# A two-layer hybrid trunk on one core: another opening and order of the recurrent stage, and attention by query blocks with its steps spread over two heads

## What is computed

```
x = x + recurrent_block(rmsnorm(x), ...)          # layer 0
x = x + sq_relu_mlp(rmsnorm(x), w1, w2)           # d_ff = 4096
kv = rmsnorm(x) @ w_kv                            # shared K and V
x = x + diff_attention(rmsnorm(x), w_q, ..., k, v)   # layer 1
x = x + sq_relu_mlp(rmsnorm(x), w1, w2)
return rmsnorm(x)
```

```
# recurrent_block: xy = h @ w_in + b_in, split in xb and yb
xc = conv4(xb) + conv_b;  r, i = sigmoid(block-diagonal matmuls of xc)
a = exp(-8 r softplus(-lam));  bx = sqrt(1 - a*a) * (i * xc)
hs = scan(a, bx);  return (hs * gelu(yb)) @ w_out
# diff_attention: 8 heads, q and k have two halves of 64 rows, v has 128
s = q k^T / 8 + ALiBi bias, causal;  p = softmax(s)
w = p[half 0] - lam * p[half 1];  o = w @ v
o = rmsnorm(o, subln_g, eps) * (1 - lam_init);  return o @ w_o
```

## Time and profile before

| | us |
|---|---|
| median of 3 runs | 1158.46 (1155.45 to 1159.59) |
| the profiled execution | 1158.65 |
| its span, first to last instruction | 1156.8 |
| PE busy | 1109.6 |
| DVE busy | 613.1 |
| ACT busy | 472.9 |
| POOL busy | 108.4 |

### The profile page before, as it was taken

How to read it: one execution, slowest core, us unless ns; L and a number is a source line. 1 busy time by engine, 2 the same in 40 slices (tenths; PEclk the granted TensorE clock), 3 DMA queues, 4 the chain that set the end, 5 groups by cost and what they waited for, 6 DMA issues and landing times.

```text
span 1156.8 us, 13824 instructions
## 1 busy us (share of the span) xinstructions
PE 1109.6 (96%) x4854; PEld 883.9 (76%) x4854; DVE 613.1 (53%) x940; ACT 472.9 (41%) x731; POOL 108.4 (9%) x95
## 2 busy tenths in 40 slices
PE   8999999999999999999999899889999999999995
PEld 4676788888888888888866566668888888888884
DVE  4676965434434434446477877866433433433434
ACT  5475754313313313434246456654422322322342
POOL 0000021000000000021013322322000000000023
PEclk8999999999999999999999999999999999999998
DMA  5222232332322232233221111123223223223322
GB/s 206 73 73 73 73 110 92 99 102 91 97 103 91 92 107 91 92 108 107 76 74 37 54 37 54 37 73 100 101 92 109 92 91 106 94 91 101 98 73 73
DMA packets 30293, 102.42 MB, mean 89 GB/s; under 512 B 3248, under 2 KB 5552, under 8 KB 30128
## 3 DMA queue, kind: packets, MB, share of 16 engines
q1 hardware_dynamic: 29968, 100.74, 26.1%
q10 hardware_dynamic: 288, 1.18, 0.3%
HBM read 99.81 MB, written 2.10 MB: 88 GB/s over the span
## 4 chain that ended last, share of the span: by engine, by line
PE 83%; DVE 10%; ACT 4%; issue 2%; DMA 1%; SPq 0%; DVEq 0%; ACTq 0%
PE ps L1249 73%; PE ps L1380 4%; ACT prob L663 2%; PE ps L1443 1%; DVE prob L1140 1%; DVE w_lo L780 1%; DVE prob L1137 1%; PE ps L1417 1%; PE ps L1308 1%; DVE lru_v L874 1%; DVE inv_lam L1135 1%; ACT w_hi L430 1%; PE ps L1313 1%; DVE lru_v L907 1%; DMA w_raw<-weights 1%
## 5 line engine op out<-in xcount | busy, mean ns | idle before, releaser
L430 ACT ACTIVATE w_hi<-w_raw 128x1024 fp32r<-128x1024 f32 x184 | 193.6, 1052 | 240.9 <-PE ps L1249 205.3
L1249 PE MATMUL ps<-h_hi,w_hi 128*128 128x512 f32 x704 | 287.9, 409 | 2.9 <-DVE w_lo L780 2.9
L1249 PE MATMUL ps<-u_hi,w_hi 128*128 128x512 f32 x696 | 279.9, 402 | 4.2 <-DVE u_lo L918 1.9
L1249 PE MATMUL ps<-h_hi,w_lo 128*128 128x512 f32 x704 | 278.0, 395 | 0.0
L1249 PE MATMUL ps<-h_lo,w_hi 128*128 128x512 f32 x704 | 277.6, 394 | 0.0
L1249 PE MATMUL ps<-u_hi,w_lo 128*128 128x512 f32 x696 | 271.1, 390 | 0.0
L1249 PE MATMUL ps<-u_lo,w_hi 128*128 128x512 f32 x696 | 271.0, 389 | 0.0
L780 DVE TENSOR_TENSOR w_lo<-w_raw,w_hi 128x1024 fp32r<-128x1024 f32 x176 | 216.7, 1231 | 29.6 <-ACT w_hi L430 29.5
L1249 PEld LDWEIGHTS ps<-h_hi,w_hi 128*128 128x128 f32 x704 | 134.4, 191 | 36.8 <-DVE w_lo L780 4.6
L1249 PEld LDWEIGHTS ps<-u_hi,w_hi 128*128 128x128 f32 x696 | 130.7, 188 | 37.8 <-issue 5.9
L1249 PEld LDWEIGHTS ps<-h_lo,w_hi 128*128 128x128 f32 x704 | 134.5, 191 | 31.8 <-issue 4.7
(11 more groups left out here) (163 smaller groups left out, 885.1 us busy)
## 6 DMA issues: line engine op xcount, KB each, us to landing
w_raw<-weights SPq DMA_DIRECT2D x184, 512.0 KB, 3.3
x<-x_t SPq DMA_DIRECT2D x8, 256.0 KB, 7.3
y_t<-att SPq DMA_DIRECT2D x8, 256.0 KB, 2.3
gw<-gate_weights ACTq DMA_DIRECT2D x1, 1024.0 KB, 5.4
lam_in<-lam_vecs ACTq DMA_DIRECT2D x1, 128.0 KB, 2.4
vec<-vectors SPq DMA_DIRECT2D x1, 64.5 KB, 4.1
```

The costliest lines, as they stand in the source:

```text
L430: nc.scalar.activation(w_hi[:, t % RING, :], w_raw[:, t % RAWS, :], ACT.Copy).then_inc(whi_done, 1)
L1249: ins = nc.tensor.matmul(ps[:, bank, :], w[:, slot, ws], o[:, k, :], start=(k == 0 and n == 0), stop=(k == NCH - 1 and n == 2))
```

## The change

Opening: `vec` is loaded from ACT's queue, and `gw` only after all chunks of `h_hi`. Tiles 0 and 1 are loaded and split in halves, interleaved with `x` chunks 0 and 1. Two of the four unused matmuls remain. The squares are added on DVE (`first_sum`), and one matmul in the middle of tile 2 adds over partitions.

Recurrent stage: the same work per chunk, in another order on ACT and DVE; gates come later among the tiles; nine more table loads on ACT. Tiles 16 to 23 split their weights before the residual add (`early=True`).

Attention: scores are one float32 product for all widths, `kq` isn't split. `combined` makes P0 + ratio P1 (ratio = -lam total0/total1) in three instructions, without the division of P0, since the norm behind it takes out a row's scale; the epsilon is scaled to match (`variance`). `attend` runs per query block with the probabilities as weights and V's 128 columns as moving data, reads V in place, and gives rows of queries; the squares are summed by ACT (`squares`), Newton runs on 128x4 on DVE, ACT scales the rows and PE turns them back with four transposes (`back`). POOL has no work here. The steps are spread: `transposes` 2 and 3, `attend` and the norm of head h-1 run during head h. All heads are written out, without loops. SBUF names: `att_hi`, `att_lo` hold the attended heads.

```
-WARM_UP = 4
+WARM_UP = 2
...
+            load_x(0)
+            load_half(0, 0)
+            load_half(1, 0)
+            load_x(1)
+            load_half(0, 1)
+            load_half(1, 1)
+            for m in range(2, NCH):
+                load_x(m)
             with sp.Fori(1, TILES // RAWS) as i:
                 for slot in range(RAWS):
...
+            nc.scalar.dma_start(gw[:, :], gate_weights).then_inc(gw_in, 16)
+            split_hi(2)
+            for m in range(4):
+                first_square(m)
+            split_hi(3)
             act.wait_ge(decay_done, 1)
             nc.scalar.activation(small[:, 1, :], small[:, 0, :], ACT.Exp, scale=-1.0).then_inc(decay_done, 1)
-            split_hi(3)
-            act.wait_ge(consts_done, 1)
-            norm_guess(N_A)
-            nc.scalar.preload_act_table_set("sigmoid_and_others")
+            for m in range(4, NCH):
+                first_square(m)
+            nc.scalar.dma_start(lam_in[:, :], lam_vecs).then_inc(lam_loaded, 16)
...
+            def scaled(h):
+                act.wait_ge(sub_rstd, h + 1)
+                if h:
+                    act.wait_ge(back_mm, h)
+                for j in range(QB):
+                    ins = nc.scalar.activation(o_rows[:, rows(j)], ps[:, BANK_O, rows(j)], ACT.Copy,
+                                               scale=o_stats[:, h % 2, 4, j:j + 1])
+                ins.then_inc(o_scaled, 1)
+            def attended_hi(h):
+                act.wait_ge(back_mm, h + 1)
+                nc.scalar.activation(att_hi[:, h, :], ps[:, BANK_T, :], ACT.Copy,
+                                     scale=lam_s[:, 6:7]).then_inc(ohi_done, 1)
...
+            def first_sum(m):
+                dve.wait_ge(sq_done, m + 1)
+                if m > 1:
+                    dve.wait_ge(sum_done, m - 1)
+                nc.vector.tensor_tensor(acc[:, :], work[:, 0, :] if m == 1 else acc[:, :],
+                                        work[:, m % 4, :], ALU.add).then_inc(sum_done, 1)
...
+            split_lo(4)
             decay()
             norm_newton(N_A)
             dve.wait_ge(conv_consts, 1)
+            split_lo(5)
             branch(0)
+            split_lo(6)
             branch(1)
+            branch(2)
             conv(0)
-            split_lo(4)
-            branch(2)
+            branch(3)
             conv(1)
+            split_lo(7)
+            branch(4)
...
+                dve.wait_ge(exp_done, QB * h + j + 1)
+                own.step(nc.vector.reciprocal(inv[:, s:s + 1], total[:, h % 2, j, 1:2]))
+                own.wait()
+                own.step(nc.vector.scalar_tensor_tensor(
+                    out=ratio[:, s:s + 1], in0=inv[:, s:s + 1], scalar=neg_lam,
+                    in1=total[:, h % 2, j, 0:1], op0=ALU.mult, op1=ALU.mult))
+                own.wait()
+                nc.vector.scalar_tensor_tensor(out=prob[:, s, 0, 0:n], in0=prob[:, s, 1, 0:n],
+                                               scalar=ratio[:, s:s + 1], in1=prob[:, s, 0, 0:n],
                                                op0=ALU.mult, op1=ALU.add).then_inc(prob_done, 1)
...
+                nc.vector.scalar_tensor_tensor(
+                    out=o_stats[:, h % 2, 1, :], in0=o_stats[:, h % 2, 0, :], scalar=1.0 / V_DIM,
+                    in1=o_stats[:, h % 2, 3, :], op0=ALU.mult, op1=ALU.add).then_inc(var_done, 1)
...
             for _ in range(WARM_UP):
@@ -1322,18 +1326,24 @@
             for k in range(NCH):
                 for t in range(2):
                     if k == 0:
-                        tile_starts(t, 0)
+                        pe.wait_ge(first_lo, t + 1)
+                    elif k == NCH // 2:
...
-            gates_after = {2: (0,), 3: (1,), 4: (2,), 5: (3,), 7: (4,), 8: (5,), 10: (6,), 11: (7,)}
+            gates_after = {4: (0,), 5: (1, 2), 6: (3,), 7: (4,), 9: (5,), 10: (6,), 12: (7,)}
...
+                    if t == 2 and k == NCH // 2:
+                        pe.wait_ge(sum_done, NCH - 1)
+                        nc.tensor.matmul(ps[:, BANK_STATS, :], ones[:, :], acc[:, :], start=True,
+                                         stop=True).then_inc(stats_done, 1)
...
-                if n == P:
-                    products = ((kq, kq),)
-                for m, (q, k) in enumerate(products):
-                    for c in range(2):
-                        rows = slice(c * HEAD_DIM, (c + 1) * HEAD_DIM)
-                        ins = nc.tensor.matmul(ps[:, BANK_SCORES + 2 * (j % 2) + c, 0:n],
-                                               q[rows, 1, qb * P:(qb + 1) * P], k[rows, 0, 0:n],
-                                               start=(m == 0), stop=(m == len(products) - 1))
+                    pe.wait_ge(bank_read, T_QK + 2 * h + 2)
+                if a >= 2:
+                    pe.wait_ge(scores_read, 2 * (a - 1))
+                for c in range(2):
+                    rows = slice(c * HEAD_DIM, (c + 1) * HEAD_DIM)
+                    ins = nc.tensor.matmul(ps[:, BANK_SCORES + 2 * (j % 2) + c, 0:n],
+                                           kq[rows, h % 2, 1, qb * P:(qb + 1) * P],
+                                           kq[rows, h % 2, 0, 0:n], start=True, stop=True)
...
+                pe.wait_ge(prob_done, a + 1)
+                if a >= 1:
+                    pe.wait_ge(trans_read, a)
+                if h and j == 2:
+                    pe.wait_ge(olo_done, O_ATT + h)
...
+            def attend(h, j):
+                a = QB * h + j
+                qb = QB - 1 - j
+                pe.wait_ge(trans_read, a + 1)
+                if h and j == 0:
+                    pe.wait_ge(o_scaled, h)
+                for kb in range(qb + 1):
+                    ins = nc.tensor.matmul(ps[:, BANK_O, qb * P:(qb + 1) * P],
+                                           prob_t[:, j % 2, kb * P:(kb + 1) * P],
+                                           value[:, kb, h * P:(h + 1) * P], start=(kb == 0),
+                                           stop=(kb == qb))
                 ins.then_inc(att_mm, 1)
-            def sub_sum(h, i):
-                pe.wait_ge(att_read, at(h + 1, i, 2))
-                bank = BANK_T if h == HEADS - 1 else BANK_O
...
+            def back(h):
+                pe.wait_ge(o_scaled, h + 1)
+                pe.wait_ge(trans_read, min(QB * (h + 1) + 2, QB * HEADS))
+                for qb in range(QB):
+                    qs = slice(qb * P, (qb + 1) * P)
+                    ins = nc.tensor.transpose(ps[:, BANK_T, qs], o_rows[:, qs], ident[:, :])
+                ins.then_inc(back_mm, 1)
...
+            for h in range(HEADS - 1):
+                kq_part(h + 1, 0)
+                scores(h, 0)
+                if h:
+                    transposes(h - 1, 2)
+                    attend(h - 1, 0)
+                scores(h, 1)
+                if h:
+                    attend(h - 1, 1)
+                kq_part(h + 1, 1)
+                scores(h, 2)
+                if h:
+                    transposes(h - 1, 3)
+                kq_part(h + 1, 2)
+                if h:
+                    attend(h - 1, 2)
+                    attend(h - 1, 3)
+                kq_part(h + 1, 3)
+                transposes(h, 0)
+                kq_part(h + 1, 4)
+                transposes(h, 1)
+                kq_part(h + 1, 5)
+                scores(h, 3)
+                kq_part(h + 1, 6)
+                if h:
+                    back(h - 1)
+                kq_part(h + 1, 7)
+            h = HEADS - 1
```

More of the change, by code:

```diff
@@ L707, in attended_hi @@
[L707 to L717 removed]
+                n = (QB - j) * P
+                act.wait_ge(trans_mm, a + 1)
@@ new lines, in _ @@
+            h = HEADS - 2
+            biased(h, 3)
+            halved(h)
+            query(h + 1)
+            combined(h, 2)
+            key(h + 1)
+            attended_lo(h - 1)
+            combined(h, 3)
+            split_lo(T_QK + 2 * h + 1 + RING)
+            h = HEADS - 1
+            biased(h, 0)
+            biased(h, 1)
+            combined(h, 0)
+            split_lo(T_QK + 2 * h + RING)
+            variance(h - 1)
+            biased(h, 2)
+            combined(h, 1)
+            sub_newton(h - 1)
```

762 lines of the change are left out of this document (343 added, 419 removed).

## The result

| | before, us | after, us |
|---|---|---|
| median of 4 runs each | 1156.95 | 1108.82 (1108.08 to 1109.4) |
| span of the profiled execution | 1156.8 | 1107.1 |
| opening, up to tile 2 | 31.9 | 19.2 |
| tiles 2 to 23 | 145.2 | 135.7 (with one statistics matmul, 0.87) |
| attention, the stretch of the earlier trace rows | 187.0 | 159.7 |

The ratio is 0.958 (95% interval 0.956 to 0.961). Against the profiled execution of before, 1158.65 us, the median is 49.8 us shorter. The forecast was 44.5 shorter, 1114 us. The traces place all of it: 22.5 us are gone at the start of the first MLP (177.32 us before, 154.84 after) and 27.3 in attention; everything between and behind has its old length within 0.1 us. The second stretch of the earlier trace rows ends at 177.10, with the last pass ahead of the MLP; to the MLP's start it is 145.4 us, so tiles 2 to 23 are 9.7 us shorter in the table's terms and not 9.5.

A forecast was written before the change was run, and what follows sets the result against it. PE, busy nearly all of the span, was taken to set the time, with gains in its waits and needless work: 1158.65 - 10.5 (opening) - 9.5 (tiles 2 to 23) - 24.5 (attention) = 1114 us, range 1107 to 1131.

The forecast's parts named there:

- likeliest case: Whole kernel: all gains come with small failures on both sides, 1108 to 1120 us, chance 0.56.
- Opening: Start up to tile 2: first pass at about 6.9 us, 31.9 us becomes 20.5 + 0.9, gain 10.5 us.
- cold start: Tiles 0 and 1: PE's first passes run at a lowered clock after idling, costing 2 to 3.4 us.
- so it isn't the bound: Opening: DVE delivers h_lo of chunk 7 by about 14 us, so PE isn't held by it.
- hidden behind tile 1 and the start of tile 2: Opening: DVE's seven sums, 0.69 us each, finish before the one statistics matmul left in tile 2.
- Tiles 2 to 23: Recurrent stage: later gates and the new order leave 2 us of waits, 145.2 becomes 135.7 us, gain 9.5.
- Attention: Attention stretch: 187.0 us becomes 154.4 + 4.6 + 3.5 = 162.5, gain 24.5 us.
- 1: Attention scores: the float32 halves run one behind the other, 17 us more, 1131 us; chance 0.11.
- 2: Recurrent stage: bound by ACT and DVE in turn, half to all of 9.5 us lost, 1119 to 1124; chance 0.14.
- 3: Attention: the norm's chain binds each head, 1 to 2 us late, giving 1121 to 1128 us; chance 0.12.
- 4: Attention: slower than before, as transposes and `back` share one bank; PE's period above 25 us; chance 0.02.
- 5: Opening: vec's small rows still land near 7 us, 3.5 us come back, 1118 us; chance 0.03.

The follow-up runs named there:

- `same_rows`: The kernel after with both halves of the attention scores computed from the same 64 rows of query and key; 1126.2 us, in a single execution.
- `more_loads`: The kernel after with eleven more loads of ACT's function table in the recurrent stage, ahead of the sigmoids; 1112.94 us, in a single execution.
- `warm_0`: The kernel after without the two unused matmuls at the start; 1108.85 us (1108.28 to 1109.2).

## Why the prediction was right, and where it wasn't

The forecast was 1114 us, the time 1108.8: inside the likeliest case (1108 to 1120), at its lower end. Each of the three terms came out larger than forecast, by 1 to 3 us. Term by term:

**Opening, 10.5 us forecast, 11.9 measured (12.7 less the statistics matmul).** First pass at 6.18 and not 6.9, since `vec` came at 3.9 us. Tiles 0 and 1 took 13.0 us against 13.6, but by other parts: the cold start of 2 to 3.4 us wasn't there in this trace (in three others of the same opening it was, some 1.6 us), and 2.1 us beyond the passes were, 1.3 of them the wait for `h_lo` of chunk 2, which the sum had at nothing ("so it isn't the bound"). That the two cancelled is luck. The step that failed is that DVE's seven sums are "hidden behind tile 1 and the start of tile 2". They do end before the statistics matmul, as forecast (22.43 against 22.58 us), but they aren't hidden: `rstd` follows the split of tile 2 on DVE by 13.9 us in nine kernels, and they and what stands behind them fill that time and set the start of the whole stage.

**Tiles 2 to 23, 9.5 forecast, 10.6 measured (145.4 to the MLP's start, 134.8 without the statistics).** I left 2 us of waits, 1.1 remained. `rstd` was there 4.4 us behind the end of tile 2 and not 1.8, as `decay` stands ahead of Newton; the later gates covered it. Table loads cost 1.28 us as in the earlier trace rows.

**Attention, 24.5 forecast, 27.3 measured.** What PE does was right: period 18.51 against 18.7, scores 3.83 a head (7.60 us beside the passes, less 1.15 for ten transposed blocks, 2.16 for ten products and 0.46 for `back`) against 3.85. The size that was off is the waits left, 3.5 us forecast, 0.55 measured; the tail was 0.17 and 0.38 us, not 1.5, since DVE's and ACT's steps were shorter than I had added up (12.5 and 11.3 us a head against 14.7 and 13). The reason was half right. I put the stretched steps down to POOL, and the runs confirm it, but I gave the distance of 21 us to the transposes an equal part. POOL's removal alone gives nine tenths, and in a head of the old order nothing was left to gain by distance (18.19 us without a gap).

**Rivals.** 1 is refuted by `same_rows`, which is that rival built, and cost 17.4 us where I had priced it at 17. 2 and 3 are refuted by the waits of after, and 2 by `more_loads`. 4 didn't come near. 5 didn't happen, and in `warm_0` a first pass 1.2 us later cost nothing.

What stays open: whether `decay`, 3.2 us of small DVE steps ahead of Newton, moved behind it would bring the 0.8 us wait for `pad` and the opening's rest. It wasn't tried. The order of the transfers in the opening stays open too: to tell 0.9 us from the spread of 1.1 would take many traces of each kernel.

## What to carry to other kernels

When an instruction of DVE is long for its size, look for the POOL instruction that ends where it ends, and move that one first: here this alone gave 24.7 us with the old order kept. When an edit moves the start of the busiest engine and the end of the stage stays, look across the runs for the instruction that keeps a constant distance to that end; here it was `rstd` on DVE, not PE. Before a difference between two traces is put down to an edit, look how far traces differ where the program is the same: here by 1.1 us in the opening. Where one engine waits for another at a written place, the place and the other engine's order have to be moved together: half of that cost 32 us, the whole gained 11.

## What the runs showed of the hardware

- DVE's steps with two SBUF inputs, and its scalings of an SBUF tile, stood still until POOL's instruction was over: 1.05 us for 128x1 elements, 0.16 alone; 1.88 for 128x512, 0.43 alone. A reciprocal (0.17) and a step that reads PSUM (0.29) didn't. I had expected a doubling.
- Float32 matmuls on two groups of 64 rows overlap fully: 512 wide, 1.13 us of records against 1.98 on the same rows.
- PE's first passes stand 0.43 us apart for some 3 us in four traces and 0.23 apart in six, with a granted clock of 1.00 in the records of all. Three of the four have two unused matmuls ahead, as the six do.
- A load of ACT's function table took 1.28 us, and the activation behind it started 1.29 to 1.30 us after the load's start; eleven more loads moved the end of the stage by 4.9 us.
